# Prompt attention of a hybrid decoder step: the two heads of a row pair in one unit, one branch at a time

## The reference, cut to what matters

```
def gqa_probs(q, k, mask, bias):
    logits = einsum('bqgrd,bkgd->bgrqk', q, k) * scale + bias
    return masked_softmax(logits, mask)
...
o = gates[..., 0] * o_cmp + gates[..., 1] * o_sel + gates[..., 2] * o_win
```

## Time and profile before

| what | value |
|---|---|
| median of 3 runs | 3621.27 us (3621.18 to 3626.32) |
| the profiled execution's own time | 3620.41 us |
| its span, first to last instruction | 3618.6 us |
| mean granted TensorE clock, share of full speed | 0.912 |
| PE busy | 3221.9 us (89% of the span) |
| DVE busy | 1359.9 us (38%) |
| ACT busy | 996.2 us (28%) |

### The profile page before, as it was taken

One profiled execution on the slowest core, in us unless ns is written; L12 is line 12 of the kernel. 1 busy time (PEld: TensorE's weight loads), 2 busy tenths in 40 slices (PEclk: granted clock), 3 DMA queues, 4 the chain that ended last, 5 costly groups with the idle time before them and its releaser, 6 DMA issues. The chain is left out here.

```text
span 3618.6 us, 59635 instructions
## 1 busy us (share of the span) xinstructions
PE 3221.9 (89%) x23371; PEld 2940.9 (81%) x23371; DVE 1359.9 (38%) x2881; ACT 996.2 (28%) x1622; POOL 55.4 (2%) x32
## 2 busy tenths in 40 slices
PE   4689998799958998999977999987996799989997
PEld 2189998778737988999945999985884698989997
DVE  2033334335415455333322333433452363543334
ACT  1032223324314233322212222322442232342222
POOL 0000000000003000000000000000000110000000
PEclk6789999899977899999978999987998698999998
DMA  3922223521134242333265333243213332422232
GB/s 69 422 80 88 87 87 118 132 82 50 33 94 120 72 145 66 88 88 88 85 273 211 88 88 88 80 148 113 53 48 87 96 90 85 130 73 87 87 88 66
DMA packets 500006, 377.48 MB, mean 104 GB/s; under 512 B 44010, under 2 KB 470400, under 8 KB 498507
## 3 DMA queue, kind: packets, MB, share of 16 engines
q1 hardware_dynamic: 490348, 361.70, 32.8%
q10 hardware_dynamic: 9472, 13.24, 1.2%
HBM read 344.10 MB, written 39.07 MB: 106 GB/s over the span
## 5 line engine op out<-in xcount | busy, mean ns | idle before, releaser
L188 DVE TENSOR_TENSOR w_lo<-w_raw,w_hi 128x1024 fp32r<-128x1024 f32 (+1 forms) x390 | 481.1, 1234 | 1089.6 <-ACT w_hi L183 1089.4
L183 ACT ACTIVATE w_hi<-w_raw 128x1024 fp32r<-128x1024 f32 (+1 forms) x390 | 405.8, 1041 | 1175.5 <-PE pa L200 597.1
L200 PE MATMUL pa<-nhi,w_hi 128*128 128x272 f32 x1408 | 294.6, 291 | 35.0 <-DVE nlo L243 28.0
L200 PE MATMUL pa<-ghi,w_hi 128*128 128x272 f32 x1408 | 291.7, 288 | 1.3 <-DVE glo L759 1.3
L200 PE MATMUL pa<-nhi,w_lo 128*128 128x272 f32 x1408 | 292.6, 289 | 0.0
L200 PE MATMUL pa<-nlo,w_hi 128*128 128x272 f32 x1408 | 292.5, 289 | 0.0
L200 PE MATMUL pg<-nhi,w_hi 128*128 128x272 f32 x1408 | 292.4, 289 | 0.0
L200 PE MATMUL pg<-nlo,w_hi 128*128 128x272 f32 x1408 | 291.8, 289 | 0.0
L200 PE MATMUL pg<-nhi,w_lo 128*128 128x272 f32 x1408 | 291.6, 289 | 0.0
L200 PE MATMUL pa<-ghi,w_lo 128*128 128x272 f32 x1408 | 290.8, 288 | 0.0
L200 PE MATMUL pa<-glo,w_hi 128*128 128x272 f32 x1408 | 290.5, 288 | 0.0
(11 more groups left out here) (342 smaller groups left out, 4969.5 us busy)
## 6 DMA issues: line engine op xcount, KB each, us to landing
ada_raw<-in_ada_w SPq DMA_DIRECT2D x96, 768.0 KB, 13.6
w_raw<-in_ffn_w_in SPq DMA_DIRECT2D x352, 192.0 KB, 2.6
w_raw<-in_w_in SPq DMA_DIRECT2D x156, 192.0 KB, 2.9
w_raw<-in_ffn_w_out SPq DMA_DIRECT2D x128, 192.0 KB, 2.5
w_raw<-in_ffn_w_in SPq DMA_DIRECT2D x176, 128.0 KB, 2.7
w_raw<-in_ffn_w_out SPq DMA_DIRECT2D x160, 128.0 KB, 2.3
w_raw<-in_w_in SPq DMA_DIRECT2D x94, 128.0 KB, 2.9
mg<-merge_gates SPq DMA_DIRECT2D x16, 544.0 KB, 4.4
```

Of the source, the lines that this page charges most:

```text
L183: act.activation(self.hi[slot][:, 0:k, :], self.raw[slot][:, 0:k, :], ACT.Copy).then_inc(self.hi_done, 1)
L188: dve.tensor_tensor(self.lo[slot][:, 0:k, :], self.raw[slot][:, 0:k, :], self.hi[slot][:, 0:k, :].bitcast(F32), ALU.subtract).then_inc(sel ...
L200: mm = pe.matmul(out[:, half, 0:HALF], w[slot][:, k0 + n, :], x[:, n, half * HALF:(half + 1) * HALF], start=(n == 0 and w is self.hi and x ...
```

## The change

A unit is now one branch of two heads: the heads `g = 0` and `g = 1` of the same `r`, which hold their q in the lower and the upper 64 rows of the same tile. An even unit does the selected branch of both heads and the compressed one, an odd unit (`recent`) the window branch. There are again 32 units, and `qi` now runs 0, 0, 1, 1, 2, 2, 3, 3.

- In `scores` the two wide products of a unit contract over rows 0 to 63 and rows 64 to 127 and go to two banks, `s0` and `s1`. The two compressed products share a bank, so the second stands after the wide ones and waits for the first (`first_cmp`).
- In `values` the two heads' products alternate; they go to the lower and the upper 64 rows of `po`. The sum over the three branches runs over both units of a pair, and only odd units have an `outputs`, which copies 128 rows.
- `turn` has the compressed transposes, two of them, in even units only, with the wait for `outputs` ahead of them; DVE's `copy_turned` runs in even units only.
- The bias of both heads is loaded together, so four loads stand at the head of the queue, and two pairs follow behind tiles 4 and 8.
- The `memset` in `maxima` is gone. Counts and widths of all other operations of a stage stay as they were.

The lines that it puts in are below, cut to their core; those that it takes away are in the functions printed above. `weigh` and `exps` change in the same way as `maxima`, by the list that `pieces` gives.

```diff
+    tz = sb("tz", [P, 2, GROUPS, SEQ], at=st)
+    sc = sb("sc", [P, 4, 2 * SEQ + 64], at=st)
+    pT = sb("pT", [P, 2, 2 * SEQ + 2 * P], at=st)
...
+    s0, s1, t0, t1, pc, po = (ps(n, 1, st) for n in ("s0", "s1", "t0", "t1", "pc", "po"))
+    pss, pts = (s0, s1), (t0, t1)
...
     def unit(u):
+        n, recent = divmod(u, 2)
+        r, qi = divmod(n, 4)
+        return r, qi, recent, P * (qi + 1), 7 + 8 * qi
+    def parts(u):
+        return 6 * (u // 2) + 4 * (u % 2)
+    def pieces(u):
+        r, qi, recent, w, nc_ = unit(u)
+        cmp = [] if recent else [(g, 2 * SEQ + 32 * g, nc_, True) for g in range(GROUPS)]
+        return cmp + [(g, g * SEQ, w, False) for g in range(GROUPS)]
...
+        def load_bias(r):
+            if r >= 2:
+                sp.wait_ge(max_done, parts(8 * (r - 1)))
+            for g in range(GROUPS):
+                sp.dma_start(tz[:, r % 2, g, :], bass.AP(rv_dram.tensor, rv_dram.offset + P - 1 + (r + g * R) * 640 * P,
+                                                         [[639, P], [1, SEQ]])).then_inc(tz_in[r % 2], 16)
...
+        for i in range(2, NT + 2):
             load_tile(i)
+            if i in (4, 8):
+                load_bias(i // 4 + 1)
         sp.wait_ge(win_out, 16 * NB)
...
     def _(pe):
         def scores(u):
+            r, qi, recent, w, nc_ = unit(u)
+            rows = [slice(g * DH, (g + 1) * DH) for g in range(GROUPS)]
+            q = [pj[rows[g], Q0 + r, qi * P:(qi + 1) * P] for g in range(GROUPS)]
             if u >= 1:
+                pe.wait_ge(max_done, parts(u))
+            cmp = lambda g: pe.matmul(pc[:, 0, 32 * g:32 * g + nc_], q[g], kct[rows[g], NB * NCMP:NB * NCMP + nc_],
+                                      start=True, stop=True)
+            if not recent:
+                cmp(0).then_inc(first_cmp, 1)
+            for g in range(GROUPS):
+                mm = pe.matmul(pss[g][:, 0, 0:w], q[g], pj[rows[g], KV0 + (4 if recent else 2), 0:w], start=True, stop=True)
+                if g == 0 or recent:
+                    mm.then_inc(s_done, 1)
+            if not recent:
+                pe.wait_ge(first_cmp, u // 2 + 1)
+                cmp(1).then_inc(s_done, 1)
         def turn(u):
+            r, qi, recent, w, nc_ = unit(u)
+            pe.wait_ge(p_done, parts(u + 1))
             if u >= 1:
                 pe.wait_ge(pt_act, u)
+            for g in range(GROUPS):
                 for t in range(qi + 1):
+                    mm = pe.transpose(pts[g][:, 0, t * P:(t + 1) * P], sc[:, u % 4, g * SEQ + t * P:g * SEQ + (t + 1) * P], ident[:, :])
+            if not recent:
+                if u >= 2:
+                    pe.wait_ge(o_done, u // 2)
+                    pe.wait_ge(pt_dve, u // 2)
+                for g in range(GROUPS):
+                    mm = pe.transpose(po[0:nc_, 0, (g + 1) * P:(g + 2) * P], sc[:, u % 4, 2 * SEQ + 32 * g:2 * SEQ + 32 * g + nc_], ident[:, :])
+            mm.then_inc(t_done, 1)
         def values(u):
+            r, qi, recent, w, nc_ = unit(u)
             pe.wait_ge(pt_act, u + 1)
+            pe.wait_ge(pt_dve, u // 2 + 1)
+            out = [po[g * DH:(g + 1) * DH, 0, 0:P] for g in range(GROUPS)]
+            if not recent:
+                for g in range(GROUPS):
+                    pe.matmul(out[g], vcn[0:nc_, NB, g * DH:(g + 1) * DH], pT[0:nc_, u % 2, 2 * SEQ + g * P:2 * SEQ + (g + 1) * P],
+                              start=True, stop=False)
+            col = 5 * P if recent else 3 * P
+            for t in range(qi + 1):
+                for g in range(GROUPS):
+                    mm = pe.matmul(out[g], kvn[:, t, col + g * DH:col + (g + 1) * DH], pT[:, u % 2, g * SEQ + t * P:g * SEQ + (t + 1) * P],
+                                   start=False, stop=(recent == 1 and t == qi))
+                    if t == qi:
+                        mm.then_inc(pv_done, 1)
...
         def maxima(u):
+            r, qi, recent, w, nc_ = unit(u)
+            i = u % 4
+            dve.wait_ge(tz_in[r % 2], 32 * (r // 2 + 1))
+            dve.wait_ge(s_done, 2 * u + 2)
             if u >= 4:
                 dve.wait_ge(t_done, u - 3)
+            for n, (g, at, width, cmp) in enumerate(pieces(u)):
+                b = tz[:, r % 2, g, SEQ - w + 31:SEQ:16] if cmp else tz[:, r % 2, g, SEQ - w:SEQ]
+                scored = pc[:, 0, 32 * g:32 * g + width] if cmp else pss[g][:, 0, 0:width]
+                dve.tensor_tensor_reduce(sc[:, i, at:at + width], scored, b, 1.0, 3 * FLOOR, ALU.add,
+                                         ALU.max, mx[:, i, n:n + 1]).then_inc(max_done, 1)
+            dve.wait_ge(max_done, parts(u + 1))
+            k = len(pieces(u))
+            dve.tensor_scalar(neg[:, i, 0:k], mx[:, i, 0:k], FLOOR, -1.0, ALU.max, ALU.mult).then_inc(neg_done, 1)
...
         def copy_turned(u):
+            r, qi, recent, w, nc_ = unit(u)
+            if recent:
+                return
             dve.wait_ge(t_done, u + 1)
             if u >= 2:
+                dve.wait_ge(pv_done, 2 * u - 2)
+            dve.tensor_copy(pT[0:nc_, u % 2, 2 * SEQ:], po[0:nc_, 0, P:3 * P]).then_inc(pt_dve, 1)
...
         def copy_turned(u):
+            r, qi, recent, w, nc_ = unit(u)
             act.wait_ge(t_done, u + 1)
             if u >= 2:
+                act.wait_ge(pv_done, 2 * u - 2)
+            for g in range(GROUPS):
+                ins = act.activation(pT[:, u % 2, g * SEQ:g * SEQ + w], pts[g][:, 0, 0:w], ACT.Copy)
+            ins.then_inc(pt_act, 1)
         def outputs(u):
+            r, qi, recent, w, nc_ = unit(u)
+            if recent:
+                act.wait_ge(pv_done, 2 * u + 2)
+                act.activation(oa[:, r, qi * P:(qi + 1) * P], po[:, 0, 0:P], ACT.Copy).then_inc(o_done, 1)
```

More of the change, by code:

```diff
@@ L1112, in attention_stage @@
             names = ("ev_done", "win_out", "tz0", "tz1", "s_done", "max_done", "neg_done", "exp_done", "w_done",
-                                     "p_done", "t_done", "pt_act", "pt_dve", "pv_done", "o_done")
+                                     "p_done", "t_done", "pt_act", "pt_dve", "pv_done", "o_done", "first_cmp")
             with stage(nc, *names) as sems, ExitStack() as st:
                 (ev_done, win_out, tz0, tz1, s_done, max_done, neg_done, exp_done, w_done, p_done, t_done, pt_act, pt_dve,
-                 pv_done, o_done) = sems
+                 pv_done, o_done, first_cmp) = sems
                 tz_in = [tz0, tz1]
[L1118 to L1125, removed]
+                tz = sb("tz", [P, 2, GROUPS, SEQ], at=st)
+                sc = sb("sc", [P, 4, 2 * SEQ + 64], at=st)
+                pT = sb("pT", [P, 2, 2 * SEQ + 2 * P], at=st)
+                mx = sb("mx", [P, 4, 4], at=st)
+                neg = sb("neg", [P, 4, 4], at=st)
+                rsum = sb("rsum", [P, 4, 4], at=st)
+                wgt = sb("wgt", [P, 4, 4], at=st)
                 pd = ps("pd", 2, st)
-                ps_sel, ps_win, pt_sel, pt_win, pc, po = (ps(n, 1, st) for n in ("ss", "sw", "ts", "tw", "pc", "po"))
-                ps_cmp, pt_cmp = pc[:, 0, 0:32], po[:, 0, P:2 * P]
+                s0, s1, t0, t1, pc, po = (ps(n, 1, st) for n in ("s0", "s1", "t0", "t1", "pc", "po"))
+                pss, pts = (s0, s1), (t0, t1)
                 block = st.enter_context(nc.Block())
@@ L1189, in values @@
                         pe.wait_ge(pt_act, u + 1)
[L1190 to L1196, removed]
@@ L1230, in maxima @@
                             dve.wait_ge(t_done, u - 3)
[L1231 to L1237, removed]
@@ L1246, in weigh @@
+                        i, k = u % 4, len(pieces(u))
+                        dve.wait_ge(exp_done, parts(u + 1))
+                        dve.tensor_scalar(wgt[:, i, 0:k], rsum[:, i, 0:k], 1e-30, None, ALU.max).then_inc(w_done, 1)
                         dve.wait_ge(w_done, 3 * u + 1)
-                        dve.reciprocal(wgt[:, i, :], wgt[:, i, :]).then_inc(w_done, 1)
+                        dve.reciprocal(wgt[:, i, 0:k], wgt[:, i, 0:k]).then_inc(w_done, 1)
                         dve.wait_ge(w_done, 3 * u + 2)
-                        gate = gn[:, qi, r + g * R:r + g * R + 17]
@@ L1250, in weigh @@
[L1250 removed]
+                        gate = gn[:, qi, r + (2 * HEADS if recent else 0):]
+                        wg = wgt[:, i, 0:k].rearrange("p (b g) -> p b g", g=GROUPS)
+                        dve.tensor_tensor(wg, wg, strided(gate, [HEADS, k // 2], [R, GROUPS]), ALU.mult).then_inc(w_done, 1)
                         dve.wait_ge(w_done, 3 * u + 3)
[L1252 to L1254 removed]
+                        for n, (g, at, width, cmp) in enumerate(pieces(u)):
+                            v = sc[:, i, at:at + width]
+                            dve.tensor_scalar(v, v, wgt[:, i, n:n + 1], None, ALU.mult).then_inc(p_done, 1)
@@ L1283, in exps @@
                     def exps(u):
-                        r, g, qi, w, nc_ = unit(u)
                         i = u % 4
@@ L1288, in exps @@
                             act.wait_ge(w_done, 3 * u - 11)
```

(23 more changed lines are left out.)

44 lines of the change are left out of this document (removed).

## The result

The changed kernel takes 3535.98 us, the median of 4 runs (3531.94 to 3540.55), against 3621.95 us for the kernel before (4 runs). The ratio is 0.9761, with a 95% interval of 0.9744 to 0.9777: 2.4% faster. The forecast was 3541 us, in a range of 3532 to 3574. The profiled execution took 3538.02 us.

A forecast was written before the change was run, and what follows sets the result against it. The attention stages were taken to last as long as PE's list of work. Savings of 17.1 + 23.3 + 0.8 - 1.2 - 0.4 = 39.6 us a layer, 79 for two, gave 3620.4 - 79 = 3541 us, range 3532 to 3574.

The forecast's parts named there:

- start and end: Both ends of each attention stage: gains and losses taken as 0, from 2 us lost to 3 us won a layer.
- the prediction's own signs of being wrong: Steady part: PE waiting for `pT`, `sc` or the weights' low part, clock below 1.00, or `first_cmp` wait in wide units.
- the steady chain over the weights' split: After odd units' half tiles: ACT, DVE and `weigh` take 3.8 us, within PE's 5.3; rival wait, 3580 us, chance 0.04.
- Two halves run side by side: Wide passes of two heads in `scores` and `values` run at once on different array halves; 3541 us, chance 0.60.
- row halves that don't overlap: Rival in `scores`: row halves do not run at once, only values gain, 24.1 us a layer; 3572 us, chance 0.08.
- nothing overlaps: Rival in `scores` and `values`: no passes run at once, 1.9 + 0.8 us a layer saved; 3615 us, chance 0.07.
- program order: Rival: passes start in program order, three rounds of four in scores, 2 n + 1 in values; 3566 us, chance 0.17.
- 0.86 + 0.427 n: `scores` of a pair of units after the change, in us; saves 0.427 n a pair, 17.1 us a layer.
- The limit by weight loads: Wide `scores`: if the halves' loads take turns, a pair needs 0.48 us; 2.6 us a layer, half taken, 1.2.
- Slower by draining at each change: Rival: each change between halves in scores and values empties the array, 0.17 us, 38 us lost a layer; 3691, chance 0.04.
- The 27 us of turning: Before the change, the rest of a layer's steady time after scores 48, values 51 and half tiles 102 us.
- a margin of 1.5 us: Weights' split chain, 3.8 us, against PE's 5.3 at n = 1; wrong by 1 us, 16 odd units a layer return 32.

The follow-up runs named there:

- Undone one at a time: Against the changed kernel, both heads' scores used the same array rows, 3568.08 us; separately, both heads' values went to the same 64 rows of `po`, 3577.95 us.
- the kernel without the wait: Other queue order, plus compressed scores at the wide bank's free end up to n = 3, without `first_cmp`, against the changed kernel; ratio 0.9737 to the kernel before.
- the kernel with the other queue: Changed kernel with loads of the third and fourth weight tile moved ahead of the second bias pair and window-row copies in SP's queue; 3529.38 us.
- both halves undone: Changed kernel with both heads' scores on the same array rows and both heads' values in the same 64 rows of `po`; 3616.16 us.
- blocks of two: Changed kernel with wide values ordered as two tiles of one head, then two of the other, and so on; 3531.44 us, one run.

## Why the prediction was right

Per layer, by the starts of undisturbed units (n = 1 to 4, four pairs of each; before 32 x 0.43 + 80 x 0.427 = 47.9 us of scores and 51.0 of values); the last two rows are what is left of the stages' and of the span's difference:

| term | forecast, us a layer | measured |
|---|---|---|
| scores, with weight loads and `first_cmp` | 17.1 - 1.2 - 0.4 = 15.5 | 47.9 - 4 x (2.96 + 3.95) = 20.3 |
| values | 23.3 | 51.0 - 4 x (2.79 + 4.24) = 22.9 |
| turn | 0.8 | 0.4 |
| all units | 39.6 | 43.6 |
| start and end | 0 (2 lost to 3 won) | +0.5 and -1.7 |
| rest of the kernel, both layers | 0 | -3.6 |

- **PE's list sets the stage: right.** The shorter list came back as time nearly one for one: 43.6 us by the pace of the units, 44.1 and 41.9 for the whole stage. DVE and ACT stayed under it. Some of the prediction's own signs of being wrong did show, in the first units of each stage alone: PE waited for `sc`, 1.0 us in layer 0 and 1.90 in layer 1, and there also for `pT` (0.46), and layer 1's clock was 0.98. They come from the late weight tile at the start, below, and not from the steady chain over the weights' split for which the prediction gave them.
- **Two halves run side by side: right, for columns and for rows.** Undone one at a time they cost 41 and 33 us of the stages. Row halves, for which the trace of before had no row, were the weaker step; they hold as the column halves do. So three of the rivals fall: row halves that don't overlap (3572), nothing overlaps (3615), and program order (3566). Program order falls by the table above: its lone round more would add 0.11 us to each unit's wide values, and those of window units come within 0.01 of the forecast.
- **The size of scores: too small.** The step that was off is "0.86 + 0.427 n" for a pair. It lets each of the two compressed products stand by itself. In fact a compressed pass runs beside the other head's wide pass: at n = 2 a selected unit has 0.22 us more than a window unit where the forecast had 0.48. With n = 1 to 4 that is 4 x (0.12 + 0.24 + 0.25 + 0.23) = 3.4 us a layer. `first_cmp` is already taken off in this: the forecast had 0.4 us for it, and the kernel without the wait showed 0.11 for each of four units.
- **The limit by weight loads, 1.2 us: not there.** A window unit's scores at n = 1 take 0.42 us, the stream of two rounds with its head, and not the 0.48 of four loads in turn. The two halves' loads overlap: the four of that unit are through in 0.30 us.

```profile
854.11 0.30 PEld L1186 LDWEIGHTS s<-pj 64*128 64x128 f32 x4 [0.20 <-issue]
```

- **Start and end at nothing: right on the whole, as the sum of two things.** The first half tile began at 767.73 us instead of 770.55 (both stages begin at 759.7), near the 3 us forecast. Then the third weight tile was late, as the text said it would be: 4.8 and 6.2 us of ACT's time. In layer 1 PE idled 0.46 and 1.90 us behind it, and the granted clock of 2494 to 2498 us was 0.50. In the kernel with the other queue both were gone, so they come from the load's place in the queue together with the earlier demand for it.
- **Slower by draining at each change: out.** Passes of two halves follow each other 0.01 us apart. The Trainium skill ("TensorEngine Tiling (Array Packing)", Key Properties) has only a change of mode drain the engine; this trace agrees: gaps of 0.17 us remain (3.2 us in 19 on line 1221), mostly where compressed values change to wide ones, and none stands between the halves.
- **The nearness of the sum is in part luck.** The two stages gave 86.0 us where 79 was forecast, mostly by the scores, and the rest of the kernel took 3.6 of it back.
- **Two slips in the working**, neither of them in the sum. The 27 us of turning are not the rest of the 217.3 us, which would be 16: they are right for all 32 units (27.0 by the starts), but the 217.3 us hold fewer. And a margin of 1.5 us that is wrong by 1 still leaves 0.5; it would have to be wrong by 2.5 to give back 32.
- **What stays open** is the 3.6 us that code outside the two stages lost in the profiled execution. The same code was, against that one execution of before, from 4.5 us longer (both halves undone) to 1.6 us shorter (blocks of two) in the other kernels, and longer in six of these eight, so it may be scatter or that one execution; no run here tells more.

## What to carry to other kernels

Where one engine's list fills a stage, price a change by that list, and take the pace of two things side by side from any place in the same kernel that already does them so, however small: four products of one other stage gave the mechanism and the size for the column halves, and the row halves, which they don't show, turned out the same. Whatever begins earlier then asks for its data earlier: look at what stands ahead of it in the queue, for about as much as was won at the start was lost again to a weight tile that was wanted 7 us sooner, while its load still stood behind the biases and the copies of window rows. Alternate the work of two halves finely; blocks of two tiles lost almost nothing, whole rows of tiles did.

## What the runs showed of the hardware that was not expected

- Passes don't start strictly in the program's order. At 860.15 a wide pass starts between the two passes of the first compressed product (860.14 and 860.27), and stands behind both in the program; since the first head's wide product would use that product's own rows, it must be the second head's. The Trainium skill ("TensorE: Matmul & The Clock Gate", Part 3, The mechanism) has matmuls start and end in program order; here the measurement differs, and decides. The reach is short: with one head's passes all ahead of the other's, the first four of eight ran alone and the loss was 0.01, 0.27 and 0.49 us at four, six and eight passes a head; a pass went ahead of three others each time.
- The same section says that weight loads overlap matmuls only where the row groups differ, though it also lets a load go ahead into a background weight buffer. The column halves of values use the same rows, each of their passes has its own load, and 16 passes take 1.03 us, 0.064 each: no time is lost to loads there either.
- After PE had been idle for 0.46 and 1.90 us within 3 us, its granted clock over the next 4 us was 0.50, the 1.2 GHz level; in the kernel with the other queue, without these waits, it was 1.00 over layer 1's whole steady part. In layer 0 PE idled for 1.0 us behind its late tile, and the clock of the steady part stayed at 1.00.
